# Two gaps in the SBUF layout of a two-block network in split fp32: x and everything behind it moved by 192 bytes

## What is computed

```python
def retention_mla_layer(x, ...):            # first block, layer 0
    h = x @ w_in                            # 1024 -> 7744
    ...                                     # retention (4 heads) and MLA attention (8 heads)
    return concat([ret_out, mla_out]) @ w_out
def moba_layer(x, ...):                     # first block, layer 1
    h = x @ w_in                            # 1024 -> 4096, 16 heads, rope, causal attention
    return (_merge(o) * silu(g)) @ w_out
x = layer_norm(DN_ALPHA * x + y, ...)       # after each of the two

def second_block(x, ...):
    proj = rmsnorm(h) @ w_in                # 1024 -> 4112: banded attention and an SSD mixer
    h = h + concat([att, ssd]) @ w_out
    h = h + square(relu(rmsnorm(h) @ w_ff1)) @ w_ff2    # 1024 -> 4096 -> 1024
    return rmsnorm(h, norm_final_w)
```

## Time and profile before

| | |
|---|---|
| median of 3 runs | 808.21 us (807.87 to 809.13) |
| profiled execution, its own time | 807.91 us |
| span of the profile | 806.1 us |
| TensorE matmul, weight load busy | 788.4 us, 693.3 us |
| VectorE, ScalarE, GpSimd busy | 516.5 us, 411.8 us, 96.7 us |
| moved by DMA | 137.43 MB, 170 GB/s in the mean |

### The profile page before, as it was taken

One profiled execution on the slowest core, in us unless ns is written; L12 is line 12 of the kernel. 1 busy time (PEld: TensorE's weight loads), 2 busy tenths in 40 slices (PEclk: granted clock), 3 DMA queues, 4 the chain that ended last, 5 costly groups with the idle time before them and its releaser, 6 DMA issues.

```text
span 806.1 us, 13073 instructions
## 1 busy us (share of the span) xinstructions
PE 788.4 (98%) x5082; PEld 693.3 (86%) x5082; DVE 516.5 (64%) x817; ACT 411.8 (51%) x613; POOL 96.7 (12%) x68
## 2 busy tenths in 40 slices
PE   9999999999999998999999899999999999999996
PEld 8998877799988886999787799899777999999995
DVE  6965557755655568467865874876756755555555
ACT  5534444453664443445764667466655544444441
POOL 2331000010100011111301207500000000000002
PEclk9999999999999999999999999999999999999999
DMA  9865644343864662675824364543317565656541
GB/s 330 314 195 178 202 157 137 97 152 106 245 212 137 190 209 77 207 221 176 255 85 135 105 209 133 183 143 120 104 54 220 186 227 179 207 169 199 176 138 52
DMA packets 76763, 137.43 MB, mean 170 GB/s; under 512 B 7072, under 2 KB 15520, under 8 KB 76704
## 3 DMA queue, kind: packets, MB, share of 16 engines
q1 hardware_dynamic: 75456, 132.15, 51.2%
q0 software_dynamic: 1248, 4.46, 1.7%
HBM read 132.80 MB, written 1.05 MB: 166 GB/s over the span
## 4 chain that ended last, share of the span: by engine, by line
PE 90%; DVE 5%; issue 2%; ACT 1%; POOL 1%; POOLq 0%; DVEq 0%; ACTq 0%
PE acc L1035 13%; PE acc L1043 13%; PE acc L1037 13%; PE acc L1036 13%; PE acc L1045 12%; PE acc L1044 12%; PE acc L1314 1%; PE acc L1348 1%; DVE w_lo L777 1%; PE acc L1191 1%; PE acc L1298 1%; PE acc L1287 1%; PE acc L1227 1%; PE acc L1183 1%; POOL v_lo L2352 1%
## 5 line engine op out<-in xcount | busy, mean ns | idle before, releaser
L777 DVE TENSOR_TENSOR w_lo<-raw,w_hi 128x1024 fp32r<-128x1024 f32 (+1 forms) x224 | 273.0, 1234 | 184.0 <-ACT w_hi L757 95.9
L1043 PE MATMUL acc<-x_hi,w_hi 128*128 128x256 f32 x840 | 240.2, 286 | 0.4 <-DVE x_lo L2135 0.4
L1045 PE MATMUL acc<-x_hi,w_lo 128*128 128x256 f32 x840 | 237.6, 283 | 0.0
L1044 PE MATMUL acc<-x_lo,w_hi 128*128 128x256 f32 x840 | 237.6, 283 | 0.0
L757 ACT ACTIVATE w_hi<-raw 128x1024 fp32r<-128x1024 f32 (+1 forms) x128 | 133.4, 1044 | 141.7 <-PE acc L1045 71.7
L747 ACT ACTIVATE w_hi<-raw 128x1024 fp32r<-128x1024 f32 x109 | 116.0, 1064 | 116.1 <-PE acc L1045 63.0
L1043 PEld LDWEIGHTS acc<-x_hi,w_hi 128*128 128x128 f32 x840 | 160.7, 191 | 3.2 <-issue 2.5
L1044 PEld LDWEIGHTS acc<-x_lo,w_hi 128*128 128x128 f32 x840 | 160.8, 191 | 0.9 <-issue 0.5
L1045 PEld LDWEIGHTS acc<-x_hi,w_lo 128*128 128x128 f32 x840 | 160.7, 191 | 0.0
L1035 PE MATMUL acc<-w_hi,cat_hi 128*128 128x512 f32 x272 | 109.0, 401 | 0.2 <-DVE w_lo L777 0.2
L1037 PE MATMUL acc<-w_hi,cat_lo 128*128 128x512 f32 x272 | 106.9, 393 | 0.0
(11 more groups left out here) (286 smaller groups left out, 914.3 us busy)
## 6 DMA issues: line engine op xcount, KB each, us to landing
raw<-in_w_ff SPq DMA_DIRECT2D x32, 1024.0 KB, 5.2
raw<-in_w_in_even SPq DMA_DIRECT2D x28, 1024.0 KB, 5.1
raw<-in_w_in_odd SPq DMA_DIRECT2D x16, 1024.0 KB, 5.6
raw<-in_w_in SPq DMA_DIRECT2D x16, 1024.0 KB, 5.6
raw<-in_w_out_even SPq DMA_DIRECT2D x12, 1024.0 KB, 5.1
raw<-in_w_out SPq DMA_DIRECT2D x4, 1024.0 KB, 5.0
raw<-in_w_in_even SPq DMA_DIRECT2D x4, 512.0 KB, 6.4
raw<-in_w_ukv_even SPq DMA_DIRECT2D x8, 256.0 KB, 3.2
```

The costliest lines, as they stand in the source:

```text
L777: ins = eng.tensor_tensor(lo, r, hi.bitcast(F32), ALU.subtract)
L1043: pe.matmul(o, wh[:, k, fs], hi[:, ka, :], start=start and f % 2 == 0, stop=False, skip_group_check=True)
L1044: pe.matmul(o, wh[:, k, fs], lo[:, ka, :], start=False, stop=False, skip_group_check=True)
L1045: ins = pe.matmul(o, wl[:, k, fs], hi[:, ka, :], start=False, stop=stop, skip_group_check=True)
```

## The change

Two tensors that nothing reads or writes are allocated. `x_gap` has 48 floats, 192 bytes, and stands in front of x_hi; `cat_gap` has 208 floats, 832 bytes, and stands behind `soft`. x_hi, x_lo, R1, R2, R3, tmp, trig, probs, turned, gated, half_neg, ssd_c, dt_sel, stats and soft move by 192 bytes, cat_hi, cat_lo, cat2_hi, cat2_lo and zb by 1,024. cst, raw, w_hi, w_lo and res stay. No instruction is added, removed or reordered.

```diff
         res = sb("res", [P, T, D])
+        sb("x_gap", [P, 48])
         x_hi = sb("x_hi", [P, KD, S], F32R)
         x_lo = sb("x_lo", [P, KD, S], F32R)
...
         soft = sb("soft", [P, PROBS, 2, 2])
 
+        sb("cat_gap", [P, 208])
         with nc.sbuf_tensor("cat_hi", [P, 24, S], F32R) as cat_hi, nc.sbuf_tensor("cat_lo", [P, 24, S], F32R) as cat_lo:
             pass
         cat2_hi = sb("cat2_hi", [P, 16, S], F32R)
```

## The result

The changed kernel takes 799.70 us (median of 4 runs, 798.99 to 800.90) against 808.67 us (807.87 to 809.35) for the kernel before on the same chip: a ratio of 0.9885 (0.9872 to 0.9899), 9.0 us faster. The forecast was 794.0 us; the result lies 0.7 us above the range. The sign of the change, the matmuls that gain and the cause of the gain came as forecast, its size did not.

What follows compares the result with a forecast made beforehand. TensorE, busy 98%, was taken as the bound: number of matmuls times spacing. From 807.9 us, -16.4 + 1.2 + 1.0 = -14.2 gave 793.7, plus 0.3 for the median: 794.0 us, range 791 to 799.

Steps and rivals of the forecast that it cites:

- Step 1: x moving over w, 256 columns: 2,520 matmuls each 6.5 ns shorter at the ranks' spacing, 16.4 us gained.
- Step 2: x stationary under w, 512 columns: 528 matmuls each 2.3 ns longer at the head tiles' spacing, 1.2 us lost.
- Steps 3 and 4: w moving over x with 256 columns, and x under v_hi and b_hi (96 matmuls): each taken as 0.
- Step 5: Constants (cst) against R, tmp and probs, some 250 matmuls: taken as 0, at worst +1.6 us.
- Step 6: New addresses for ScalarE, VectorE, GpSimd and transfers: costed at nothing, covered by slack of 36% and more.
- Step 7: Weights' split has room; softmax chain may set the MoBA pipeline's pace: 0 to 1.9 us lost, 1.0 taken.
- rival one: Stages with little cover (first 384, MoBA 288, some 240 around turns) give gain back in waits: 798.9 us; chance 0.12.
- Rival two: Address modulo 1,024 is not the cause, perhaps nearness; x stays at 120.0 ns: 808.2 to 809.4 us; chance 0.06.
- Rival three: 192 bytes apart is a bad place; x's matmuls take 2.3 ns more everywhere: 7.0 us, 815.2 us; chance 0.06.

Runs made afterwards that it cites:

- w192: Kernel before with 192 bytes in front of w_hi instead of x_hi, 832 kept in front of cat: 809.46 us, ratio 1.0006.
- place16: Kernel before with w 16 bytes past a multiple of 32, x and cat 192 bytes past w: 791.81 us, ratio 0.9783.
- after_again: The changed kernel run once more without an edit: 800.91 us, ratio 0.9889 to the kernel before.
- x512: Kernel before with gaps of 512 bytes in front of x and 512 in front of cat: 809.09 us, ratio 1.0001.
- m1_sweep: Bare matmuls, none of the reference's work, distances 0 to 992 bytes in steps of 32: 113.3 to 120.0 ns for 256 columns, repeating every 256 bytes.
- m5_starts: Bare matmuls at distances 192, 112 and 0 behind four kinds of start: at 192 both 113.3 and 117.8 ns, at 112 all 113.3, at 0 all 120.0.
- m2_fine: Bare matmuls, distances in steps of 8 bytes behind three kinds of start: 113.3 ns behind all three at 112, behind two at 192, behind one at 16.
- m6_place: Bare matmuls at distances 0, 112 and 192, both tiles moved together: values repeat, with few exceptions, every 32 bytes; 192 at 16 past gives 113.3 and 226.7 ns.

## Why the prediction was right or wrong

**The bound** was right: the time is matmuls times spacing, the spacing depends on which tiles meet, and the earlier trace rows against the earlier trace rows is an effect of address. w192 shows that for a move of 192 bytes it is the pair that counts: with w moved along, x moving over w stays at 120.0 ns and the ranks lose their 113.3.

**Step 1 failed, by its size.** "At the ranks' spacing each is 120.0 - 113.5 = 6.5 ns shorter" took one rate for all 2,520 matmuls. It gave 10.4 us in place of 16.4. At distance 192 there are two steady rates, 113.3 and 117.8 ns, and 1,176 matmuls ran at the second: 1,176 x 4.5 = 5.3 us of the missing 6.0. The steady rate of the others is 113.3 and not 113.5, which gives 0.4 us back, and 1.2 us more go into the starts of the stretches: all that the distances exceed their steady rate adds up to 3.2 us before and 4.5 after. In the run from 355 us (357 us before), behind the first, the distances are 114, 123, 118 and then 113.3 ns after, and 119, 119, 121, 116, 118 and then 120 before; in the feed-forward runs the first five distances still take 116 to 123 ns. place16, with no stretch in the second state, gains 14.5 us on this line, so even at its best the step was worth 2 us less than the sum had it. The ranks' run, 120 matmuls without a break in one place, could show neither: it is a single stretch, which happened to stand at 113.5 ns.

**Step 2** came out: +1.2 us forecast, +1.1 measured. It too took one rate where there are two. In the first profile 48 of the 528 stood at 233.3 ns, in after_again 264 did, and there the line costs 2.0 us more than before. The five such stretches in the traces at distance 192 all stand behind x matmuls at 117.8 ns, but not every token stretch behind such matmuls is slow: retention's 216 in the first profile are not.

**Steps 3 and 4**, 0: the kinds together moved by +0.5 us here and by -1.0 in after_again. Part of the +0.5 is one stretch: from 450 to 462 us the mean granted clock was 0.89 in the changed kernel's profile, so part of the time at the lower of its two levels, and some of those matmuls lie in it; before, it was 1.00 from 445 to 470 us. **Step 5**, 0, with a bound of +1.6: all others together +0.3 us. **Step 6**, 0: VectorE 517.5 us for 516.5, ScalarE 411.7 for 411.8, and nobody waits more for them.

**Step 7 and rival one** were wrong in their mechanism. The 1.0 us that step 7 set aside was not lost in waits. No split came late: TensorE's waits sum to 11.3 us for 11.1 before, the MoBA pipeline's 288 matmuls ran without a gap at 117.8 ns, and in place16 they ran at 113.5 without a gap too. It was a likeness that misleads: rival one named the first 384 and the MoBA 288 as the stages that would not gain, and these are indeed slow, but not because they wait. That its 798.9 us lies only 0.8 us from the measured time is luck. The prediction's own test tells them apart: "TensorE's waits above some 12 us in all, or the MoBA pipeline no shorter". The pipeline is shorter by 2.2 ns for each matmul, a third of the 6.7 that a fast stretch gains, which no wait explains.

**Rival two** is wrong in its form (nearness) and right in a detail: the address modulo 1,024 is not the measure, modulo 256 is. x512, with a shift of two times 256, changes nothing. **Rival three** is wrong: no x stretch of the changed kernel settled above 117.8 ns.

**The sum.** -10.4 + 1.1 + 0.5 + 0.3 + 0.3 (the head tiles) = -8.2 us, against -8.1 of the two spans.

The rule that the prediction weighed, from the Trainium skill, page "TensorE: Matmul & The Clock Gate", section "Part 2: What happens when you issue a matmul" (two independent read ports, so loading weights takes no bandwidth from the running matmul), does not agree with m1_sweep as it stands: with no other engine at work and a weight load beside every matmul, 256 columns cost 113.3 to 120.0 ns by how the two operands stand to each other.

Two things stay open. The traces show that distance and place count, not what inside the chip makes them count. And what picks the state at distance 192 behind a pause or a float32 matmul was not found: six of eight and five of eight came out fast. In m5_starts the stretches that settle at 117.8 ns stand at 117 to 119 from the second distance on, while the others pass through some distances between 114 and 123 first; that tells the states apart early, but not what picks one. Of the ten slow stretches of the changed kernel, the MoBA run stands behind b_hi over x_lo, a pair at distance 0, as the small kernel would have it. The other nine stand behind small products in float32, where the small kernel shows both states, and so does the changed kernel: of the four short stretches behind L1316, those from 373.1 and 411.0 us are fast and those from 377.2 and 402.7 slow.

## What to carry to other kernels

Where TensorE is the bound and every matmul brings a new stationary tile, read the spacing from start to start for each pair of tiles, and give the two tiles' starts modulo 256 bytes a place in the layout: in this split fp32r kernel it was worth 2.2% for no instruction. Look for it with a sweep of bare matmuls, not with one lucky stretch of the kernel, and sweep the pair's own place too, and what runs in front of the stretch. A spacing read off one uninterrupted stretch is a rate of that stretch; before multiplying it by all matmuls, ask what the many starts do, and whether other stretches of the same form hold another rate.

## What the runs showed of the hardware

- A matmul of 256 fp32r columns with a fresh stationary tile each time costs 113.3 to 120.0 ns by the distance of its operands in steps of 32 bytes (m1_sweep; one stretch at another distance, 104 bytes in m2_fine, took 130), with a period of 256 bytes; 512 columns cost 226.7 to 240 ns (m1_sweep, m6_place). With w at a multiple of 32 the distances that are good differ: 112 and 192 for 256 columns, 0 for 512.
- The pair's own place counts with a period of 32 bytes: distance 112 has 113.3 ns at 0 and 116.7 to 120.0 at 16, distance 192 has both layouts at their best at 16 (m6_place, place16).
- At distance 192, with w at a multiple of 32, the same instructions have two steady rates, 113.3 and 117.8 ns for 256 columns and 228.9 and 233.3 ns for 512. Where a stretch of 256 columns follows 512-column matmuls without a break, the byte offset that these read went with the rate in m5_starts: 8 of 8 fast behind 192, 0 of 8 behind 0. Behind a wait of 0.4 us the same stretch was fast in one execution and slow in another.
- The weight load changes with the state: its mean over the x matmuls is 191 ns before, 188 to 189 after, 188 in place16, and in the 117.8 ns state one load in three takes 192 ns. It is a mark of the state and no measure of the spacing: in three of the six feed-forward runs of before the distances go round in 118, 121, 120, 124, 117 ns with loads of 189 ns, in the other three they are 120 flat with loads of 192, and the mean is 120 in both. So more than one pattern was there to be seen before the change, at no cost.
